# Hybrid mixer and MoE step on one core: the convolution state's load is issued later, the second gate's tiles are done in split products, the layer norm sums on VectorE, and VectorE's order in the mixer is laid out anew

## The chip, the cores and the metric

The kernel runs on one core of a Trainium2 chip. The metric is the device time of one execution in microseconds (us). Three executions of the kernel before took 702.01, 702.13 and 704.56 us; the median is 702.13 us. A further execution was profiled: 702.46 us, of which 700.6 us lie between its first and its last instruction.

The engines are called as the profile calls them: PE (TensorE), DVE (VectorE), ACT (ScalarE), POOL (GpSimd), SP (SyncE, which only issues transfers here). SPq, ACTq and so on are the transfers that an engine issues.

## The reference

One step of a decoder trunk on 272 prompt rows (16 meta tokens and 256 prompt tokens) and 8 sample sequences of 4 tokens: T = 304 tokens, 1024 channels.

```python
xn = rmsnorm(x, norm1_g)
u_x, u_y, c_v, c_g, g_rnn, g_conv = split(xn @ w_in)          # w_in is 1024 x 6144
xc  = causal_dwconv(u_x, state_rglru_conv, width 4)
r, i = sigmoid(blockdiag(xc, w_rg_a) + b_rg_a), sigmoid(blockdiag(xc, w_rg_i) + b_rg_i)
a = exp(-8 r softplus(-lambda));  h = scan(a, sqrt(1 - a*a) * i * xc, state_rglru_h)
rnn_out = (h * gelu(u_y)) @ w_rnn_proj
glu = c_v * sigmoid(c_g)
cc  = causal_dwconv(glu, state_conformer_conv, width 31)
conv_out = silu(layernorm(cc, conf_ln_g, conf_ln_b)) @ w_conv_proj
x = x + (sigmoid(g_rnn) * rnn_out + sigmoid(g_conv) * conv_out) @ w_out
x = x + moe(rmsnorm(x, norm2_g))                               # 4 groups x 8 experts, 2 of a group
y = rmsnorm(x, final_norm_g)
```

It returns y and the new states of the scan and of both convolutions.

## The kernel before

Everything up to `w_out` is the mixer; channels lie on the partitions, 128 at a time, so a tensor is 8 channel tiles (KT) of 304 tokens. A **tile** `(k, c)` is one 128 x 304 output of a 1024-row weight. There are 64, in this order: `cv 0, cg 0, ..., cv 7, cg 7` (the two halves of the GLU), then eight each of `ux`, `uy`, `gr`, `gc` (the two output gates), `rp` (`w_rnn_proj`) and `cp` (`w_conv_proj`). They cycle through four PSUM banks; a tile waits until the one four places ahead has been read (`tile_act` for ACT's, `glu_done` and `tile_dve` for DVE's). The weights come in blocks of 2 MB (four tiles) through four places in the buffer `ring`, loaded by SP when the tiles of the block four ahead are done (`load_block`).

Tiles up to `gc` are eight fp32 products each (L1426). Those of `rp` and `cp`, and `w_out` behind them, are **split products**: a weight half-block of two tiles is rounded by ACT into `w_hi` (`weight_high(u)`, L625), DVE subtracts to get `w_lo` in the weight's own place (`weight_low(u)`, L1009), the input is split likewise (`gel_hi`, `gel_lo`; `cc_hi`, `cc_lo`; `mrg_hi`, `mrg_lo`), and PE does three fp32r products for each of the eight input tiles (L1421). `w_hi` has three places (HI_SLOTS), so `weight_high(u)` waits for the two tiles of `u - 3`.

**Start.** SP issues x, half of the first weight block, eight small parameters and the rest of that block, then block 1. ACT issues five small parameter loads and, as fourth of six, the 0.96 MB `state_conformer_conv` into `crow` (L522; 1920 pieces of 512 bytes); then it computes the row norms. PE transposes the parameters (waits `par_in`), the convolution state (`conf_states`, waits `cst_in`) and the normalized x (L1386), whose copies into `xnT` let the first tile begin. DVE copies the transposed state into `glu` (L885) before its copies of `xnT`, then computes the softplus of lambda (`lam`).

**DVE's order** is written out by hand: `old_samples(c)` does the window products of the sample sequences with the old state (four products and a sum), `gate(c)` makes one channel tile of `glu` from the tiles `cv c` and `cg c`, `conv_prompts(c)` does the 30 taps (L952) of two channel tiles, `conv_rnn` the width-4 convolution, `variance` and `scans` the recurrence. Parts of one stand between taps of another (`between`). PE's `gates(c)` (the block-diagonal products, L1438) wait for `conv_rnn`.

**Layer norm.** The mean of `cc` over channels is eight fp32 products with a matrix of 1/1024, before tile `rp 1` (L1462); the mean of the squares is eight more, before `rp 5` (L1467). DVE and ACT subtract, square, take the root, normalize, apply silu and split.

After the mixer, 32 experts pass in order, each with its 3 MB of weights loaded, split and multiplied.

## Time and profile before

| | before |
|---|---|
| median of three executions | 702.13 us |
| profiled execution, of which its span | 702.46 us, 700.6 us |
| PE busy | 641.0 us, 91% |
| DVE busy | 513.2 us, 73% |
| ACT busy | 356.2 us, 51% |
| mean share of DMA engines in 380 to 700.6 us | 0.80 |

The times of the trace are from the start of the span. The profile counts an fp32 product as two MATMUL instructions and an fp32r product as one, so a tile of eight fp32 products is "x16" and one of split products is "x24". The clock granted to PE stands as a share of full speed, 1.00 or about 0.50.

### The profile page before, as it was taken

What the parts mean: (1) busy time and instruction counts of PE and PEld (TensorE: products, weight loads), DVE (VectorE), ACT (ScalarE), POOL (GpSimd) and SP (SyncE); (2) the same over time, 40 slices, a digit from 0 to 9 for tenths busy, and PEclk for the clock granted to TensorE, in tenths of its full rate; (3) what the DMA queues carried; (4) which work ended last, traced back from release to release, by engine and by line L of the source; (5) the groups of instructions that cost most, each with busy time, mean ns of one, the idle gap of its engine ahead of it and who ended that gap; (6) DMA issues with size and microseconds to landing.
All of it is one profiled execution on the core that took longest, in us unless ns stands there. A gap on an engine that the chain in (4) does not pass through costs nothing.

```text
span 700.6 us, 7972 instructions
## 1 busy us (share of the span) xinstructions
PE 641.0 (91%) x2872; PEld 468.4 (67%) x2872; DVE 513.2 (73%) x783; ACT 356.2 (51%) x511; POOL 81.7 (12%) x78
## 2 busy tenths in 40 slices
PE   4499999999999989999998899999999999999930
PEld 4366677777777779997788566666666666666610
DVE  0479999998861864864469888888888888888506
ACT  2121111147612304644355877777777777777522
POOL 1000000022240000020000031111111111111110
PEclk9699999999999999999999999999999999999985
DMA  9482615333333333504071889999999999997114
GB/s 226 158 292 48 220 42 199 121 120 121 120 121 120 121 121 120 153 2 181 1 303 58 340 330 363 361 359 375 369 370 366 377 374 368 357 372 270 37 64 156
DMA packets 45717, 150.20 MB, mean 214 GB/s; under 512 B 9990, under 2 KB 13302, under 8 KB 33062
## 3 DMA queue, kind: packets, MB, share of 16 engines
q1 hardware_dynamic: 38112, 144.56, 55.8%
q10 hardware_dynamic: 3974, 2.54, 1.4%
q0 software_dynamic: 3584, 2.50, 1.1%
q8 instruction: 25, 0.41, 0.2%
q14 instruction: 22, 0.18, 0.1%
HBM read 145.51 MB, written 15.02 MB: 229 GB/s over the span
## 4 chain that ended last, share of the span: by engine, by line
PE 68%; DVE 9%; ACT 2%; DMA 2%; issue 1%; SPq 0%; ACTq 0%; POOLq 0%; DVEq 0%
PE bank L1607 25%; PE bank L1632 14%; PE bank L1426 11%; PE bank L1421 7%; PE bank L1517 5%; DVE work L952 2%; PE bank L1574 2%; DMA ring<-expert_rows 1%; PE bank L1619 1%; PE bank L1489 1%; ACT work L674 1%; PE bank L1467 1%; PE bank L1462 1%; DVE work L976 1%; DVE x L1335 1%
## 5 line engine op out<-in xcount | busy, mean ns | idle before, releaser
L1426 PE MATMUL bank<-work,ring 128*128 128x304 f32 x768 | 198.7, 419 | 3.6 <-DVE work L912 2.7
L1426 PEld LDWEIGHTS bank<-work,ring 128*128 128x128 f32 x768 | 145.6, 190 | 54.8 <-DVE work L912 3.7
L1244 DVE TENSOR_TENSOR lo_gu<-ring,hi_gu 128x2048 fp32r<-128x2048 f32 x64 | 143.8, 2288 | 39.7 <-ACT hi_gu L762 39.7
L762 ACT ACTIVATE hi_gu<-ring 128x2048 fp32r<-128x2048 f32 x64 | 118.6, 1901 | 0.0
L952 DVE SCALAR_TENSOR_TENSOR work<-work,par 128x272 f32<-128x272 f32 x240 | 108.2, 524 | 0.4 <-ACT work L585 0.3
L1607 PE MATMUL bank<-hi_gu,xe_hi 128*96 128x512 f32 x256 | 102.4, 400 | 0.6 <-ACT work L786 0.6
L1607 PE MATMUL bank<-hi_gu,xe_lo 128*96 128x512 f32 x256 | 100.5, 393 | 0.0
L1607 PE MATMUL bank<-lo_gu,xe_hi 128*96 128x512 f32 x256 | 100.4, 392 | 0.0
L1632 PE MATMUL bank<-ring,windows 128*96 128x512 f32 x128 | 65.2, 590 | 0.0
L1009 DVE TENSOR_TENSOR w_lo<-ring,w_hi 128x2048 fp32r<-128x2048 f32 x12 | 28.0, 2341 | 35.4 <-ACT w_hi L625 35.4
L1607 PEld LDWEIGHTS bank<-lo_gu,xe_hi 128*96 128x96 f32 x256 | 41.3, 162 | 17.6
L1607 PEld LDWEIGHTS bank<-hi_gu,xe_hi 128*96 128x96 f32 x256 | 42.3, 165 | 16.2 <-ACT work L786 0.8
L1607 PEld LDWEIGHTS bank<-hi_gu,xe_lo 128*96 128x96 f32 x256 | 41.4, 162 | 15.4
L800 ACT ACTIVATE gate_weights<-bank,rs_col 96x256 f32<-96x256 f32 x32 | 15.1, 472 | 59.2 <-PE bank L1607 59.1
L494 POOL DMA_INDIRECT expert_rows<-outst,row_i x16 | 25.6, 1602 | 157.9 <-ACT outst L780 157.9
L625 ACT ACTIVATE w_hi<-ring 128x2048 fp32r<-128x2048 f32 x12 | 22.9, 1912 | 40.5 <-PE bank L1421 29.0
L1244 DVE TENSOR_TENSOR lo_dn<-ring,hi_dn 128x1024 fp32r<-128x1024 f32 x32 | 39.0, 1219 | 2.1 <-ACT hi_dn L767 2.1
L1632 PE MATMUL bank<-hi_dn,hT_hi 128*96 128x512 f32 x64 | 38.0, 594 | 2.5 <-ACT outst L780 1.5
L494 POOL DMA_INDIRECT expert_rows<-work,row_i x16 | 22.6, 1410 | 111.2 <-ACT work L780 111.2
L767 ACT ACTIVATE hi_dn<-ring 128x1024 fp32r<-128x1024 f32 x32 | 34.1, 1066 | 0.0
L565 ACT ACTIVATE ring<-bank 128x304 f32<-128x304 f32 x8 | 3.4, 424 | 58.0 <-PE bank L1426 58.0
L1244 DVE TENSOR_TENSOR xe_lo<-work,xe_hi 128x768 fp32r<-128x768 f32 x32 | 30.4, 949 | 1.0 <-issue 0.9
(271 smaller groups left out, 946.9 us busy)
## 6 DMA issues: line engine op xcount, KB each, us to landing
ring<-w_exp_gate SPq DMA_DIRECT2D x32, 1024.0 KB, 6.8
ring<-w_exp_up SPq DMA_DIRECT2D x32, 1024.0 KB, 9.2
ring<-w_exp_down SPq DMA_DIRECT2D x32, 1024.0 KB, 9.7
ring<-w_in SPq DMA_DIRECT2D x11, 2048.0 KB, 8.4
ring<-w_rnn_proj SPq DMA_DIRECT2D x2, 2048.0 KB, 7.9
ring<-w_conv_proj SPq DMA_DIRECT2D x2, 2048.0 KB, 7.9
ring<-w_out SPq DMA_DIRECT2D x2, 2048.0 KB, 7.9
ring<-w_in SPq DMA_DIRECT2D x2, 1024.0 KB, 13.3
```

Of the source, the lines that this page charges most:

```text
L494: nc.gpsimd.indirect_dma_start(out=rows, out_offset=bass.IndirectOffsetOnAxis(ap=row_i[0:C, e:e + 1], axis=0), in_=row_st[e % 2], in_offse ...
L625: nc.scalar.activation(hi, w, ACT.Copy).then_inc(whi_done, 1)
L762: nc.scalar.activation(hi_gu[e % 2][:, k], w_gu[s][:, k], ACT.Copy).then_inc(ehi_gu, 1)
L767: nc.scalar.activation(hi_dn[e % 2], w_dn[s][:, 0], ACT.Copy).then_inc(ehi_dn, 1)
L952: ins = vec.scalar_tensor_tensor(y, glu[:, ch, w:w + TP], pcw[:, w, ch:ch + 1], y, ALU.mult, ALU.add)
L1009: vec.tensor_tensor(part, value, as_f32(high), ALU.subtract).then_inc(lo_sem, 1)
L1244: vec.tensor_tensor(part, whole, as_f32(high), ALU.subtract).then_inc(out_done, 1)
L1421: ins = mm(bank[m % 4][:, 0:T], w[:, i, cols], xp[i], start=(i == 0 and j == 0), stop=(i == KT - 1 and j == 2))
L1426: ins = mm(bank[m % 4][:, 0:T], mix_w[b % MIX_SLOTS][:, i, (c % MB) * P:(c % MB + 1) * P], xnT[:, i], start=(i == 0), stop=(i == KT - 1))
L1517: ins = mm(bank[q][0:ROWS[t]], xp[:, c, tok], w[:, i], start=(c == 0 and j == 0), stop=(c == KT - 1 and j == 2))
L1607: ins = mm(bank[b][0:C], xp[b][:, k], w[:, k], start=(k == 0 and j == 0), stop=(k == KT - 1 and j == 2))
L1632: ins = mm(bank[4 + n][0:C], hp, w[:, at], start=(j == 0), stop=(j == 3))
```

## The change

- The load of `state_conformer_conv` moves on ACT from its fourth transfer to behind the row norms' square root. PE transposes the state after tile 0 instead of before the transposes of x, and DVE copies it into `glu` behind `lam` instead of before `xnT`.
- The eight `gc` tiles become split products: `first_split` and `first_tile` begin at `gc`, so there are four more half-blocks, and the unit numbers of all later ones grow by four. ACT makes `xn_hi`, DVE `xn_lo` (in the place of `xnT`).
- The layer norm's sums over the eight channel tiles are two `tensor_reduce` on DVE (`csum`), each followed by one fp32 product: the first before `gc 7`, the second before `rp 3`. Subtraction and square are one instruction each instead of two.
- `old_samples`, `gate` and the taps stand in another order, and the split and `rp` steps behind them as well.

```diff
--- before.py
+++ after.py
...
+        xn_lo = chan(rounded("xn_lo", "work", 0, KT * T))
...
+        xn_hi = [rounded(f"xn_hi{c}", *(("gate_weights", 2 * KT * P - (HB - c) * T) if c < HB else
+                                        ("ring", MIX_SLOTS * BLOCK_WORDS + (c - HB) * T)), T) for c in range(KT)]
...
+        csum = cv4[0][:, 0:T]
...
-        first_split, first_tile = blocks.index(("rp", 0)), tile_at["rp", 0]
+        first_split, first_tile = blocks.index(("gc", 0)), tile_at["gc", 0]
         WO_UNIT = 2 * (blocks.index(("wo", 0)) - first_split)
...
-            act.dma_start(crow[0:120], a["state_conformer_conv"][0].rearrange("s r (c p) -> (s r c) p", p=P)
-                          .rearrange("(i q) p -> q i p", i=16)).then_inc(cst_in, 16)
             act.dma_start(prow[64:72, 3], a["norm2_g"][0].rearrange("(c p) -> c p", p=P)).then_inc(par_in, 16)
             act.dma_start(prow[0:96, 4:6], a["state_rglru_conv"][0].rearrange("s r (c p) -> (s r c) p", p=P)
                           .rearrange("(i q) p -> q i p", i=2)).then_inc(par_in, 16)
...
             nc.scalar.activation(stat[:, 3:6], stat[:, 3:6], ACT.Sqrt).then_inc(rs_done, 1)
+            act.dma_start(crow[0:120], a["state_conformer_conv"][0].rearrange("s r (c p) -> (s r c) p", p=P)
+                          .rearrange("(i q) p -> q i p", i=16)).then_inc(cst_in, 16)
 
...
+                if (k, c) == ("gr", 0):
+                    weight_high(0)
+                    weight_high(1)
+                if (k, c) == ("gr", 1):
+                    act.wait_ge(gate_mm, KT)
+                    for i in range(KT):
+                        nc.scalar.activation(xn_hi[i], xnT[:, i], ACT.Copy).then_inc(xhi_done, 1)
+                if (k, c) == ("gr", 3):
+                    weight_high(2)
                 if k == "gc" and c in (1, 3, 5):
-                    weight_high(c // 2)
+                    weight_high(c // 2 + HI_SLOTS)
...
-            weight_high(3)
-            for q in range(2):
-                half = slice(q * HB, q * HB + HB)
-                act.wait_ge(cen_done, q + 1)
-                nc.scalar.activation(sq[:, half], cc[:, half], ACT.Square).then_inc(sq_done, 1)
-            weight_high(4)
+            act.wait_ge(cen_done, 1)
+            nc.scalar.activation(sq, cc, ACT.Square).then_inc(sq_done, 1)
+            weight_high(6)
             act.wait_ge(var_done, 1)
             nc.scalar.activation(sq[:, 0], sq[:, 0], ACT.Sqrt).then_inc(std_done, 1)
-            weight_high(5)
+            weight_high(7)
...
-            weight_high(6)
+                if c == HB:
+                    weight_high(8)
+            weight_high(9)
+            weight_high(10)
...
@@ -878,11 +892,6 @@
             dve.wait_ge(rst_T, 1)
             vec.tensor_copy(state_cols(ux, UXP, UXS)[:, :, 0:RW - 1],
                             bank[1][:, 0:192].rearrange("p (s r c) -> p s r c", s=NS, r=RW - 1)).then_inc(rst_done, 1)
-            for s in range(NS):
-                dve.wait_ge(cst_T, s // 2 + 1)
-                at = GLP + s * GLS
-                b = bank[4 + s // 2][:, 240 * (s % 2):240 * (s % 2) + 240]
-                vec.tensor_copy(glu[:, :, at:at + CW - 1], b.rearrange("p (r c) -> p c r", c=KT)).then_inc(cst_done, 1)
...
+            for s in range(NS):
+                dve.wait_ge(cst_T, s // 2 + 1)
+                at = GLP + s * GLS
+                b = bank[4 + s // 2][:, 240 * (s % 2):240 * (s % 2) + 240]
+                vec.tensor_copy(glu[:, :, at:at + CW - 1], b.rearrange("p (r c) -> p c r", c=KT)).then_inc(cst_done, 1)
...
                     dve.wait_ge(cstep, 2 * c)
+                else:
+                    dve.wait_ge(cst_done, NS)
...
-            for c in range(3):
-                old_samples(c)
+            old_samples(0)
+            old_samples(1)
             gate(0)
-            for c in range(3, 6):
-                old_samples(c)
+            old_samples(2)
+            old_samples(3)
             gate(1)
-            conv_prompts(0, between={4: lambda: old_samples(6), 5: lambda: gate(2), 10: lambda: old_samples(7),
-                                     13: lambda: gate(3), 22: lambda: gate(4)})
-            conv_prompts(2, between={1: lambda: gate(5), 10: lambda: gate(6), 18: lambda: gate(7), 24: new_samples})
+            old_samples(4)
+            old_samples(5)
+            gate(2)
+            conv_prompts(0, between={10: lambda: gate(3), 12: lambda: old_samples(6), 16: lambda: gate(4),
+                                     20: lambda: old_samples(7), 23: lambda: gate(5)})
+            conv_prompts(2, between={2: lambda: gate(6), 12: lambda: gate(7), 24: new_samples})
...
-            conv_prompts(6, between={12: lambda: weight_low(0), 18: lambda: weight_low(1), 24: lambda: weight_low(2)})
+            def tokens_low():
+
+                dve.wait_ge(tile_mm, first_tile)
+                for c in range(KT):
+                    low(xn_lo[:, c], xnT[:, c], xn_hi[c], xhi_done, xlo_done, c)
+
+            conv_prompts(6, between={6: lambda: weight_low(0), 10: lambda: weight_low(1), 16: lambda: weight_low(2),
+                                     22: tokens_low})
             vec.memset(spare, 1.0).then_inc(conv_done, 1)
             for c in range(KT):
                 low(gel_lo[:, c], gel[:, c], gel_hi[:, c], ghi_done, glo_done, c)
+
+            for i in range(KT):
+                dve.wait_ge(tap_done[i % 2], (i // 2 + 1) * (CW - 1))
+            dve.wait_ge(smp_done, 1 + 2 * TS)
+            vec.tensor_reduce(csum, cc.rearrange("p c n -> p n c"), AX_X, ALU.add).then_inc(sum_done, 1)
...
+            weight_low(3)
+            weight_low(4)
+            dve.wait_ge(mean_mm, 1)
+            vec.tensor_tensor(cc, cc, bank[4][:, 0:T].unsqueeze(1).broadcast_to([P, KT, T]), ALU.subtract)\
+               .then_inc(cen_done, 1)
+            weight_low(5)
+            dve.wait_ge(sq_done, 1)
+            vec.tensor_reduce(csum, sq.rearrange("p c n -> p n c"), AX_X, ALU.add).then_inc(sum_done, 1)
+            weight_low(6)
             tile("rp", 0)
-            dve.wait_ge(mean_mm, 1)
-            for q in range(2):
-                half = slice(q * HB, q * HB + HB)
-                vec.tensor_tensor(cc[:, half], cc[:, half], bank[4][:, 0:T].unsqueeze(1).broadcast_to([P, HB, T]), ALU.subtract)\
-                   .then_inc(cen_done, 1)
             tile("rp", 1)
-            weight_low(3)
-            tile("rp", 2)
-            tile("rp", 3)
-            tile("rp", 4)
             dve.wait_ge(var_mm, 1)
             vec.tensor_scalar(sq[:, 0], bank[5][:, 0:T], EPS, None, ALU.add).then_inc(var_done, 1)
             dve.wait_ge(std_done, 1)
             step(vec.reciprocal(sq[:, 0], sq[:, 0]))
             for c in range(KT):
                 vec.tensor_tensor(cc[:, c], cc[:, c], sq[:, 0], ALU.mult).then_inc(nrm_done, 1)
-            tile("rp", 5)
-            weight_low(4)
-            tile("rp", 6)
+            tile("rp", 2)
+            tile("rp", 3)
+            weight_low(7)
+            tile("rp", 4)
...
             for c in range(KT):
                 low(cc_lo[:, c], cc[:, c], cc_hi[:, c], chi_done, clo_done, c)
-                if c == 3:
-                    tile("rp", 7)
-            weight_low(5)
-            weight_low(6)
+                if c == 2:
+                    tile("rp", 5)
+                if c == HB:
+                    weight_low(8)
+                    tile("rp", 6)
+            tile("rp", 7)
+            weight_low(9)
+            weight_low(10)
             for c in range(KT):
...
-                    weight_low(c // 2 + 7)
...
-            pe.wait_ge(cst_in, 16)
-            for g in range(4):
-                conf_states(g)
...
                     x_hi, x_lo, ready = {"rp": (rows(gel_hi), rows(gel_lo), glo_done),
-                                         "cp": (rows(cc_hi), rows(cc_lo), clo_done)}[k]
+                                         "cp": (rows(cc_hi), rows(cc_lo), clo_done)}.get(k, (xn_hi, rows(xn_lo), xlo_done))
...
-                if (k, c) == ("rp", 1):
+                if (k, c) == ("gc", 7):
+                    pe.wait_ge(sum_done, 1)
                     pe.wait_ge(st_ev, 2)
-                    pe.wait_ge(smp_done, 1 + 2 * TS)
-                    for i in range(KT):
-                        pe.wait_ge(tap_done[i % 2], (i // 2 + 1) * (CW - 1))
-                        ins = mm(bank[4][:, 0:T], ones_d, cc[:, i], start=(i == 0), stop=(i == KT - 1))
-                    ins.then_inc(mean_mm, 1)
-                if (k, c) == ("rp", 5):
-                    for i in range(KT):
-                        pe.wait_ge(sq_done, i // HB + 1)
-                        ins = mm(bank[5][:, 0:T], ones_d, sq[:, i], start=(i == 0), stop=(i == KT - 1))
-                    ins.then_inc(var_mm, 1)
+                    mm(bank[4][:, 0:T], ones_d, csum, start=True, stop=True).then_inc(mean_mm, 1)
+                if (k, c) == ("rp", 3):
+                    pe.wait_ge(sum_done, 2)
+                    mm(bank[5][:, 0:T], ones_d, csum, start=True, stop=True).then_inc(var_mm, 1)
                 tile(m)
+                if m == 0:
+                    pe.wait_ge(cst_in, 16)
+                    for g in range(4):
+                        conf_states(g)
```

PE's instructions from its first products to the tiles. In the kernel before L1361 and L1364 transpose parameters, L1369 the convolution's state, L1386 x, and L1426 is a tile's product:

```order
L1364 MATMUL bank<-ident,ring 128x96 x2
L1369 MATMUL bank<-ident,ring 128x120 x16
L1386 MATMUL bank<-ident,ring 128x128 x2
L1386 MATMUL bank<-ident,ring 128x48
...
L1426 MATMUL bank<-work,ring 128x304 x176
```

In the changed kernel (L1406 is the state, L1419 x, L1459 a tile's product):

```order
L1401 MATMUL bank<-ident,ring 128x96 x2
L1419 MATMUL bank<-ident,ring 128x128 x2
L1419 MATMUL bank<-ident,ring 128x48
...
L1459 MATMUL bank<-work,ring 128x304 x8
L1406 MATMUL bank<-ident,ring 128x120 x16
L1459 MATMUL bank<-work,ring 128x304 x168
```

The state's 16 transposes moved behind the eight products of tile 0.

DVE's instructions from the last scan to the first `rp` tile, before (L952 is a tap, L1009 a low part, L1047 to L1054 copy states, L1004 reads a tile of `rp`):

```order
L995 SCALAR_TENSOR_TENSOR work<-ring 128x312 x4
L952 SCALAR_TENSOR_TENSOR work<-work,par 128x272 x30
L1009 TENSOR_TENSOR w_lo_62<-ring,w_hi_66 128x8x256
L952 SCALAR_TENSOR_TENSOR work<-work,par 128x272 x12
L1009 TENSOR_TENSOR w_lo_62<-ring,w_hi_67 128x8x256
...
L952 SCALAR_TENSOR_TENSOR work<-work,par 128x272 x14
L1042 MEMSET spare 128x1
L1009 TENSOR_TENSOR gel_lo<-work,gel_hi 128x304 x8
L1047 COPY outst<-bank 96x256
...
L1004 TENSOR_TENSOR work<-bank,work 128x304
```

In the changed kernel (L969 is a tap, L1026 a low part, L1076 the first sum, L1079 the first state copy, L1092 the subtraction of the mean, L1096 the second sum):

```order
L1012 SCALAR_TENSOR_TENSOR work<-ring 128x312 x4
L969 SCALAR_TENSOR_TENSOR work<-work,par 128x272 x18
L1026 TENSOR_TENSOR w_lo_65<-ring,w_hi_67 128x8x256
...
L969 SCALAR_TENSOR_TENSOR work<-work,par 128x272 x12
L1026 TENSOR_TENSOR xn_lo<-work,xn_hi_81 128x304
...
L969 SCALAR_TENSOR_TENSOR work<-work,par 128x272 x18
L1069 MEMSET spare 128x1
L1026 TENSOR_TENSOR gel_lo<-work,gel_hi 128x304 x8
L1076 TENSOR_REDUCE conv<-work 128x304
L1079 COPY outst<-bank 96x256
...
L1026 TENSOR_TENSOR w_lo_66<-ring,w_hi_67 128x8x256
L1026 TENSOR_TENSOR w_lo_63<-ring,w_hi_68 128x8x256
L1092 TENSOR_TENSOR work<-work,bank 128x2432
L1026 TENSOR_TENSOR w_lo_63<-ring,w_hi_69 128x8x256
L1096 TENSOR_REDUCE conv<-work 128x304
```

The first low part of a weight stands 12 taps earlier, the eight of `xn` stand before the last 18 taps, and between the low parts of `gel` and the two low parts of weights for `gc 6`, `gc 7` and `rp 0` there is now the first sum.

## Rows read from the trace of the kernel before

**Rows 1.** The page's first part: busy time of each engine.
```profile
PE 641.0 (91%) x2872; PEld 468.4 (67%) x2872; DVE 513.2 (73%) x783; ACT 356.2 (51%) x511; POOL 81.7 (12%) x78
```
**Rows 2.** Windows: length, busy PE, PEld, DVE, ACT, POOL, clock, DMA share, GB/s.
```profile
380.00:700.60 320.60, 289.53 (x1197) 188.90 (x1195) 239.95 (x211) 230.13 (x305) 48.39 (x33) 0.96 0.80 306
```
**Rows 3.** The chain that ended last: start, us, what.
```profile
157.36 1.47 DVE ring L983
...
213.73 24.58 PE bank L1426 x96
...
249.41 5.13 PE bank L1421 x24
254.54 4.09 PE bank L1462 x16
258.63 13.44 PE bank L1421 x96
...
314.75 15.29 PE bank L1517 x66
```
**Rows 4.** Timeline of the start: start, us, engine line op names shapes xcount [idle before <-releaser].
```profile
3.19 7.37 ACTq L524 DMA_DIRECT2D ring<-norm_g  x1
...
13.72 1.28 ACT L531 ACT_TABLE_LOAD   x1 [13.72 <-issue]
...
18.71 0.21 ACT L544 ACTIVATE stat<-stat 128x3 f32<-128x3 f32 x1 [0.23 <-DVE stat L867]
...
19.16 2.07 DVE L873 TENSOR_SCALAR ring<-x,stat 128x1024 f32<-128x1024 f32 x3
...
26.96 0.95 PE L1361 MATMUL bank<-ident,ring 96*128 96x96 f32 x4 [17.01 <-DMA ring<-state_rglru_conv]
...
28.03 3.38 PE L1369 MATMUL bank<-ident,ring 120*128 120x120 f32 x16
...
31.23 4.50 PE L1386 MATMUL bank<-ident,ring 128*128 128x128 f32 x24
...
36.65 23.52 PE L1426 MATMUL bank<-work,ring 128*128 128x304 f32 x91 [0.92 <-ACT work L549]
...
41.75 2.16 DVE L921 TENSOR_TENSOR windows<-work,par 128x248 f32<-128x248 f32 x4
```
**Rows 5.** Transfers of 0 to 30 us: queue with packets, MB, share; issue with us to landing.
```profile
q1 hardware_dynamic: 2608, 5.47, 61.6%
q10 hardware_dynamic: 2539, 1.26, 21.3%
...
ring<-w_in SPq DMA_DIRECT2D x1, 2048.0 KB, 20.1
ring<-state_conformer_conv ACTq DMA_DIRECT2D x1, 960.0 KB, 23.0
...
x<-x_sample SPq DMA_DIRECT2D x1, 128.0 KB, 9.6
```
**Rows 6.** Timeline of PE: the longer of its two stalls among the first tiles.
```profile
63.08 16.64 PE L1426 MATMUL bank<-work,ring 128*128 128x304 f32 x64 [1.64 <-DVE work L912]
```
**Rows 7.** Timeline of DVE and ACT behind the last scan.
```profile
187.34 17.10 DVE L952 SCALAR_TENSOR_TENSOR work<-work,par 128x272 f32<-128x272 f32 x30
224.21 2.29 DVE L1009 TENSOR_TENSOR w_lo<-ring,w_hi 128x2048 fp32r<-128x2048 f32 x1 [19.76 <-ACT w_hi L625]
226.42 5.04 DVE L952 SCALAR_TENSOR_TENSOR work<-work,par 128x272 f32<-128x272 f32 x12
...
234.56 0.80 ACT L643 ACTIVATE gel_hi<-work 128x304 fp32r<-128x304 f32 x2
```
**Rows 8.** Groups of DVE by shape: busy us, mean ns.
```profile
L925 DVE TENSOR_REDUCE work<-windows 128x32 f32<-128x992 f32 x8 | 9.5, 1186 | 0.3
...
L1112 DVE TENSOR_TENSOR halves<-x,halves 128x512 fp32r<-128x512 f32 x4 | 4.5, 1138 | 0.0
...
L1098 DVE TENSOR_TENSOR x<-bank,x 128x512 f32<-128x512 f32 x4 | 2.7, 685 | 4.2 <-PE bank L1517 4.2
```

More of the change, by code:

```diff
@@ L230, in trunk @@
         stat, spare = sb("stat", 21), sb("spare", 1)
-        (par_in, first_in, cst_in, wbd_in, router_in, g_in, consts, zeros, dconst, dstep, astep, pstep, rstep,
+        (xhi_done, xlo_done, par_in, first_in, cst_in, wbd_in, router_in, g_in, consts, zeros, dconst, dstep, astep, pstep, rstep,
          ss_done, ms_done, rs_done, xn_done, par_T, par_done, rst_T, rst_done, cst_T, cst_done, xT_done, xnT_done, xnT_act,
@@ L236, in trunk @@
          gate_mm, gate_act, dec_done, vsq_done, vrt_done, inp_done, scan_done, gelu_done, prod_done,
-         st_cp, st_T, st_ev, st_out, mean_mm, cen_done, sq_done, var_mm, var_done, std_done, nrm_done, silu_done,
+         st_cp, st_T, st_ev, st_out, mean_mm, cen_done, sq_done, sum_done, var_mm, var_done, std_done, nrm_done, silu_done,
          merged, wo_mm, x1_done, ss2_done, ms2_done, rs2_done, xT2_mm, pad_done, ss_half, xT2_act, xT2_dve,
@@ L243, in trunk @@
          y_out) = (sem(n) for n in (
-            "par_in first_in cst_in wbd_in router_in g_in consts zeros dconst dstep astep pstep rstep "
+            "xhi_done xlo_done par_in first_in cst_in wbd_in router_in g_in consts zeros dconst dstep astep pstep rstep "
             "ss_done ms_done rs_done xn_done par_T par_done rst_T rst_done cst_T cst_done xT_done xnT_done xnT_act "
@@ L247, in trunk @@
             "gate_mm gate_act dec_done vsq_done vrt_done inp_done scan_done gelu_done prod_done "
-            "st_cp st_T st_ev st_out mean_mm cen_done sq_done var_mm var_done std_done nrm_done silu_done "
+            "st_cp st_T st_ev st_out mean_mm cen_done sq_done sum_done var_mm var_done std_done nrm_done silu_done "
             "merged wo_mm x1_done ss2_done ms2_done rs2_done xT2_mm pad_done ss_half xT2_act xT2_dve "
@@ L701, in _ @@
             for c in range(1, KT + 1, 2):
-                weight_high(c // 2 + 7)
+                weight_high(c // 2 + 11)
                 for i in (c - 1, c):
@@ L705, in _ @@
                     nc.scalar.activation(mrg_hi[:, i], sgr[:, i], ACT.Copy).then_inc(mhi_done, 1)
-            weight_high(11)
+            weight_high(15)
             load_table(ACT.Sqrt)
@@ L1085, in _ @@
                 if c % 2:
-                    weight_low(c // 2 + 7)
+                    weight_low(c // 2 + 11)
                 if c >= 2:
@@ L1090, in _ @@
                 low(mrg_lo[:, c], sgr[:, c], mrg_hi[:, c], mhi_done, mlo_done, c)
-            weight_low(11)
+            weight_low(15)
             def residual(n, t):
```

## The prediction

> **What bounds the kernel now.** PE is busy 91% of the span [rows 1], so I read its gaps and the chain of waits, stage by stage. The timeline of the start comes first: PE transposes nothing until 26.96 us, when the last parameter lands, and its first tile starts at 36.65 [rows 4]. From there the chain runs over DVE up to 157.36 + 1.47 = 158.83 us [rows 3] (taps and recurrence; PE's gates wait for it), and PE stalls now and then for `gate`, 1.64 us at the longest [rows 6]. Then PE leads: `gc` from 213.73, `rp` from 249.41, `cp` up to 314.75, where `w_out` begins [rows 3]. In that stretch DVE had room: it stood 19.76 us before its first low part of a weight [rows 7]. From 380 us on the experts keep PE busy 289.5 of 320.6 us [rows 2]; nothing changes there, their loads start when mixer tiles end, and a gain before simply moves them. So the sum has two terms: how much earlier DVE's chain starts, and how much shorter `gc` to `cp` becomes.
>
> **The start.** The state's load fills ACT's queue: the tiny transfer behind it takes 7.37 us to issue, ACT computes only from 13.72, and the last parameter, two transfers behind, lands at 26.96 [rows 4]. Without it five small issues remain, done at about 4 us (estimate). What then sets the pace:
> - x. Its last part landed 9.6 us after its issue [rows 5], at 12.3 us. ACT's queue took 21.3% of 30 us x 16 engines for 2539 packets, 40 ns each; SP's took 61.6% for 2608, 113 ns each [rows 5]. The state's 1920 packets are 4.8 us of all engines; I take 1.8 of these out before x: 10.5 us. ACT and DVE needed 21.23 - 15.00 = 6.2 us from the table load to the end of the normalized x [rows 4]; two of the three squares (1 us each, estimate) now pass while x arrives, so it is ready at 10.5 + 4.2 = 14.7, the root at about 12.4.
> - Parameters. SP's eight stand behind x and half a block, 2.2 of 5.47 MB, or 7.4 of its 18.5 us; with ACT's other 619 packets (1.5 us), a start at 2.5 and about 2 us to land I take 14 us. Ends: 10.5 (with x) and 26.96 (no gain).
> - PE. 1.07 us of parameters [rows 4], about 1 us until DVE has copied them, then the 36.65 - 31.23 = 5.4 us of x less the 1 us that its first two channel tiles overlap: tile 0 from 20.5 to 24.6.
> - The state, issued at 12.4, is then the last. The same load took 23.0 us while ACT's queue served 2539 packets, of which it was 1920: 23.0 x 1920 / 2539 = 17.4 us. Two packets of 40 and 113 ns in turn on 16 engines give 9.6 ns x 1920 = 18.4. I take 17.6, landing at 30.0. Ends: inside tile 0 (by 24.6) and 12.4 + 23.0 = 35.4.
> - PE waits 5.4 us, transposes the state in 31.23 - 28.03 = 3.2 us [rows 4] and starts tile 1 at 33.2 instead of 36.65 + 4.09 = 40.7. Block 1, whose load took 20.1 us [rows 5] and was issued at 7.3, is there. DVE copies the last state 0.9 us later and begins `old_samples` at 34.1 instead of 41.75 [rows 4]: **7.6 us earlier**. `lam` (3.4 us) ends by then, hidden under the wait; if the state came early, up to 2 us of it would show.
>
> [...]
>
> **The order of `old_samples`, `gate` and taps.** The same instructions. Counting in tiles of 4.09 us from tile 1, each `gate` now stands before PE needs its bank, so the stalls (1.64 and a shorter one) go. But PE then waits that much at `gates(0)` for `conv_rnn`: DVE's chain is the same length, and the cost is 0. If DVE met a `gate` too soon it would lose at most 0.4 us each.
>
> **`gc` to `cp`.** All times here are on the clock of before; 7.6 comes off afterwards. On PE alone the change is large: a split tile takes 13.44 / 4 = 3.36 us against 4.09 (eight: 5.8), and two times eight sum products of 4.09 (there are two such rows) become two of 0.51 (7.2). But the order on DVE and ACT decides.
> - DVE from 187.34: 18 taps. POOL works beside it until 200, and the 30 taps took 17.10 instead of 12.5 [rows 7]; I put all of the 4.6 before 200, so the 18 end at 199.1. Then three low parts at 2.2 (starts follow each other 0.08 before an end) and 32 taps at 0.42 [rows 7], 20.0: DVE begins `xn_lo` at 219.1. ACT's `w_hi` and `xn_hi` are done by 199. PE was ready at 213.73 and waits 5.8.
> - `gc 0` takes 5.13 as the first `rp` tile did after its wait of 3 us (249.41 less 213.73 and eight tiles) [rows 3]: 224.7. `gc 1` to `5`: 241.5.
> - `gel_lo`. ACT makes the last two `gel_hi` behind its reading of `gc 4` (238.1), 0.4 + 0.8 [rows 7]: 239.3, `gel_lo` ends 239.8. Then the first sum, 1.7 us of state copies and one low part of 2.25 stand before `gc 6`.
> - The sum reads 2432 values with a stride of 304. Lower end: TENSOR_REDUCE took 1186 ns for 992 in a row [rows 8], so 2.9 us. The only strided pass over SBUF of which the trace has a twin is L1112, 1138 ns against 685 for 512 [rows 8], about 2.1 ns a value: 5.2 us. Upper end, with no row: twice that per value on top of the reduce, 8. I take 5.2, since the stride is the nearest likeness.
> - So the weights for `gc 6` come at 239.8 + 5.2 + 1.7 + 2.25 = 249.0; PE waits 7.5, `gc 6` takes 5.1 (to 254.1), mean product and `gc 7` 3.9: `rp` starts at 258.0 instead of 249.41, 8.6 us late.
> - `rp`. Before 5.13 + 7 x 3.36 + 2 x 4.09 = 36.8, to 286.3; now 8 x 3.36 + 0.5 = 27.4, to 285.4. The layer norm must keep up. Mean at 254.6; subtraction 2.7, square 2.3, second sum 5.2: 264.8; a low part and two `rp` tiles on DVE: 268; the product before `rp 3` at 268.1. From variance to the last `cc_lo` took 13.5 us before and gets one more weight split (1.9): 284. It fits with 1 us to spare.
> - `cp`. Before it ended at 314.75, 28.45 after `rp`, 1.5 of them waits for `cc_lo`. Now 8 x 3.37 = 27.0: 312.4. **Gain 2.3 us.**
>
> [...]
>
> **Sum.** 702.46 - 7.6 - 2.3 = 692.6 for an execution like the profiled one; its time lies 0.3 above the median, so **692.3 us**. Ends: the state's landing moves it by +5.4 to -5.4, the sums by -2.3 to about +4.6 (below).
>
> **Rivals.**
> - A. The state lands within tile 0. Tile 1 at 27.8: 5.4 us less, 687. For: block and x drain before, leaving room. [...]
> - B. The state takes 23.0 again, behind block 2 as well: 5.4 us more, 697.7.
> - C. DVE keeps up in `gc`, the PE arithmetic counts in full: 5.8 + 7.2 + 2.3 + 1.7 for the wait and slow tile before `rp` = 17, plus the start: 677.5. Against: the order on DVE, step by step above; the 19.76 us of room lie before the weights' split, but `gel_lo` and the sum stand after `gc 4`.
> - D. Slower: the sums are dearer than any row. The first moves `gc 6` one to one; the second, beyond 6.2 us, uses up the layer norm's spare 1 us and counts too. At r us each: 692.3 + 1 + 2 (r - 6.2). At 10.6 us (4.4 ns a value) the gain is gone; at 12.5 us it is 706. For: nothing measured has this stride. Against: the dearest strided row is 2.2 ns.
>
> **How the numbers follow.** Forecast 0.56 (its own range 688 to 697), A 0.14, B 0.12, C 0.04, D 0.10 (most of it with 7 to 11 us, 695 to 703), the rest unnamed. The range 684.5 to 700 takes in A and B with their own spread and leaves out C, half of D and the unnamed. A measurement here tells about 0.5%, 3.5 us, from no change: faster (under 698.6) 0.86, same 0.09, slower 0.05.
>
> **What would show it.** Tile 0 at 20 to 21 us, state transposes at 30, `old_samples` at 34; no stall among the first tiles, one of 2 us at the gates; PE idle some 6 us before `gc 0` and 7 before `gc 6`; TENSOR_REDUCE of about 5.2 us twice; no gap between `rp 7` and `cp 0`. It is wrong if tile 0 starts after 24 us, the state lands outside 27 to 33, or the sums are outside 4 to 6.2 us.

## The result, and the profile after

The changed kernel takes 693.5 us (median of 4 runs, 692.93 to 693.88) against 702.43 for the kernel before (4 runs, 702.01 to 704.56); the ratio is 0.9866, with a 95% interval of 0.9845 to 0.9888. 692.3 was predicted. The profiled execution took 693.58 us, with a span of 691.8.

The start first. The view is the timeline of the kernel after (start, us, engine line op names shapes xcount, and in brackets the idle time before with its releaser); it answers to [rows 4]. L1391 are products whose results nobody reads: 24 of them keep PE busy at the start.
```profile
1.58 7.74 PE L1391 MATMUL bank<-ident 128*128 128x128 f32 x48 [1.58 <-POOL ident L444]
...
12.93 0.34 ACTq L548 DMA_DIRECT2D ring<-state_conformer_conv  x1
...
15.48 0.95 PE L1398 MATMUL bank<-ident,ring 96*128 96x96 f32 x4 [6.17 <-DMA ring<-rg_lambda]
...
16.55 7.11 PE L1419 MATMUL bank<-ident,ring 128*128 128x128 f32 x24
24.58 6.97 PE L1459 MATMUL bank<-work,ring 128*128 128x304 f32 x16 [0.92 <-ACT work L554]
31.39 1.80 PE L1406 MATMUL bank<-ident,ring 120*128 120x120 f32 x16
33.03 17.31 PE L1459 MATMUL bank<-work,ring 128*128 128x304 f32 x67
...
34.72 2.16 DVE L938 TENSOR_TENSOR windows<-work,par 128x248 f32<-128x248 f32 x4
```
PE gets the parameters at 15.48 instead of 26.96 and DVE begins `old_samples` at 34.72 instead of 41.75: 7.03 us. But x's transposes take 7.11 us where they took 4.50, and tile 0 6.97 where one takes 4.09; nothing stands before the state's transposes. Tile 0's eight fp32 products stand there as x16. The windows of the same kernel say why (busy time of PE, PEld, DVE, ACT, POOL, then the granted clock, DMA share, GB/s):
```profile
10.00:15.00 5.00, 0.00 (x0) 0.00 (x0) 1.97 (x5) 2.39 (x5) 0.00 (x0) 0.79 1.05 337
15.00:20.00 5.00, 4.52 (x18) 2.87 (x18) 2.50 (x5) 0.51 (x1) 0.00 (x0) 0.50 1.06 357
20.00:25.00 5.00, 4.08 (x14) 2.31 (x14) 1.07 (x2) 1.95 (x5) 0.00 (x0) 0.50 1.03 200
25.00:30.00 5.00, 5.00 (x11) 3.30 (x11) 2.90 (x17) 2.58 (x3) 0.00 (x0) 0.51 1.22 340
30.00:35.00 5.00, 5.00 (x30) 4.10 (x30) 2.89 (x9) 0.00 (x0) 0.00 (x0) 1.00 0.62 224
```
The granted clock is 0.50 from 15 to 30 us, and 0.79 on average in the 5 us before; PE had stood idle for the 6.17 us before the parameters. In windows of 0.25 us from 5 to 40 us it is 1.00 or 0.50, here and in the kernel before, with other values only where it changes (0.72 and 0.64 here, 0.89 and 0.97 before); a value in between for 5 us is an average of the two. The state had been issued at 12.93 and, by the view of the transfers, took:
```profile
ring<-state_conformer_conv ACTq DMA_DIRECT2D x1, 960.0 KB, 16.4
```
It landed at 29.3, behind the slow tile 0.

Then `gc` to `cp`: first what PE waited for between 15 and 310 us (us in total, times, longest), then the chain that ended last (`gc 0` to `4`, `gc 6`, `w_out` and the group that is read below), which answers to [rows 3].
```profile
PE bank L1454 <- DVE w_lo L1026: 6.6, 1, 6.6
PE bank L1454 <- DVE xn_lo L1026: 6.2, 1, 6.2
...
PE bank L1471 <- DVE work L993: 2.5, 1, 2.5
```
```profile
212.90 19.16 PE bank L1454 x120
...
241.97 4.95 PE bank L1454 x24
...
304.95 19.48 PE bank L1549 x84
...
345.60 4.08 PE bank L1521 x24
```
PE waits 6.2 us for `xn_lo` before `gc 0`, 6.6 for the weight's low part before `gc 6`, and `w_out` begins at 304.95 instead of 314.75, 9.80 us earlier; 9.9 was predicted. The tiles behind these two waits are slow as well: the first five of `gc` take 19.16 us where five of 3.36 would take 16.8, with a granted clock of 0.50 in their first 4.8 us and 1.00 from there, and `gc 6` (x24, three fp32r products for each of eight input tiles) takes 4.95, at 0.70 on average. DVE's timeline shows what stood before that low part:
```profile
207.34 5.04 DVE L969 SCALAR_TENSOR_TENSOR work<-work,par 128x272 f32<-128x272 f32 x12
212.29 3.17 DVE L1026 TENSOR_TENSOR xn_lo<-work,xn_hi 128x304 fp32r<-128x304 f32 x8
215.37 7.51 DVE L969 SCALAR_TENSOR_TENSOR work<-work,par 128x272 f32<-128x272 f32 x18
...
224.63 0.86 DVE L1026 TENSOR_TENSOR gel_lo<-work,gel_hi 128x304 fp32r<-128x304 f32 x2 [1.56 <-ACT gel_hi L657]
...
231.34 0.86 DVE L1026 TENSOR_TENSOR gel_lo<-work,gel_hi 128x304 fp32r<-128x304 f32 x2 [4.29 <-ACT gel_hi L657]
...
233.67 4.38 DVE L1076 TENSOR_REDUCE conv<-work 128x304 f32<-128x2432 f32 x1
...
239.56 4.47 DVE L1026 TENSOR_TENSOR w_lo<-ring,w_hi 128x2048 fp32r<-128x2048 f32 x2
```
From 223 to 233 DVE stands 7.2 us idle before `gel_lo` in four waits (1.56, 0.69, 4.29, 0.69), and only then sums.

The spans differ by 8.8, not 9.8. The last 1.0 us goes in the routing stretch: the transposes of the second half of x take 4.08 us in the chain above, and in the kernel before, in the same view:
```profile
355.40 3.18 PE bank L1489 x24
```
The instructions are the same. The windows of 5 us that begin 40 us behind `w_out`'s start hold this group and show a lower granted clock (first before, then after):
```profile
354.75:359.75 5.00, 4.62 (x35) 4.14 (x35) 2.11 (x9) 3.74 (x8) 0.74 (x1) 0.92 0.97 370
```
```profile
344.95:349.95 5.00, 4.62 (x29) 4.04 (x29) 1.35 (x5) 3.74 (x8) 0.22 (x1) 0.74 1.00 365
```
The group is 0.9 of the 1.0 us. In the kernels below it took 3.18 to 4.32 us; in runs 5, 8, 9 and 12 it took 3.18, but twelve products of `w_out` that end some 5 us before it took 4.41 to 4.54 us instead of 2.98, and in run 1 both were slow. I found no reason for it, so I compare the kernels by `w_out`'s start as well as by their time.

### The profile page after: what moved, and what is told of

It reads as the page before. It is cut to its first block, busy times and chain, and to the rows that moved or that the text cites. A ratio compares the mean times of both kernels' runs of the same rounds, so it can differ in the third digit from the quotient of the medians.

```text
span 691.8 us, 8085 instructions
## 1 busy us (share of the span) xinstructions
PE 634.8 (92%) x2908; PEld 470.6 (68%) x2908; DVE 532.8 (77%) x796; ACT 365.4 (53%) x522; POOL 82.7 (12%) x78
## 4 chain that ended last, share of the span: by engine, by line
PE 61%; DVE 8%; DMA 2%; ACT 1%; issue 1%; SPq 0%; ACTq 0%; POOLq 0%; DVEq 0%
PE bank L1639 26%; PE bank L1664 14%; PE bank L1454 12%; PE bank L1549 5%; DVE work L969 3%; PE bank L1606 2%; DVE w_lo L1026 1%; DMA ring<-expert_rows 1%; PE bank L1521 1%; PE bank L1651 1%; DVE conv L1076 1%; DVE x L1372 1%; DMA expert_rows<-work,row_i 0%; DVE x L1362 0%; PE bank L1511 0%
## 5 line engine op out<-in xcount | busy, mean ns | idle before, releaser
L1459 PE MATMUL bank<-work,ring 128*128 128x304 f32 x640 | 169.1, 426 | 0.9 <-ACT work L554 0.9
L1459 PEld LDWEIGHTS bank<-work,ring 128*128 128x128 f32 x640 | 123.8, 194 | 44.7 <-issue 3.6
L969 DVE SCALAR_TENSOR_TENSOR work<-work,par 128x272 f32<-128x272 f32 x240 | 107.7, 523 | 0.2
L1639 PEld LDWEIGHTS bank<-lo_gu,xe_hi 128*96 128x96 f32 x256 | 41.3, 162 | 17.7
L1026 DVE TENSOR_TENSOR w_lo<-ring,w_hi 128x2048 fp32r<-128x2048 f32 x16 | 37.0, 2321 | 12.5 <-ACT w_hi L630 12.5
L630 ACT ACTIVATE w_hi<-ring 128x2048 fp32r<-128x2048 f32 x16 | 30.5, 1910 | 24.3 <-PE bank L1454 11.9
L1454 PE MATMUL bank<-xn_hi,w_hi 128*128 128x304 f32 x64 | 21.5, 335 | 12.8 <-DVE w_lo L1026 6.6
```

What stands on the lines that cost most here:

```text
L630: nc.scalar.activation(hi, w, ACT.Copy).then_inc(whi_done, 1)
L969: ins = vec.scalar_tensor_tensor(y, glu[:, ch, w:w + TP], pcw[:, w, ch:ch + 1], y, ALU.mult, ALU.add)
L1026: vec.tensor_tensor(part, value, as_f32(high), ALU.subtract).then_inc(lo_sem, 1)
L1454: ins = mm(bank[m % 4][:, 0:T], w[:, i, cols], xp[i], start=(i == 0 and j == 0), stop=(i == KT - 1 and j == 2))
L1459: ins = mm(bank[m % 4][:, 0:T], mix_w[b % MIX_SLOTS][:, i, (c % MB) * P:(c % MB + 1) * P], xnT[:, i], start=(i == 0), stop=(i == KT - 1))
L1639: ins = mm(bank[b][0:C], xp[b][:, k], w[:, k], start=(k == 0 and j == 0), stop=(k == KT - 1 and j == 2))
```

## The experiments

Theory 1: the start gives about 7 us; the single products for the norm sums pay; the split of the gate tiles pays nothing, because DVE's order turns its saving on PE into waits and slow tiles behind them. Against it: all gain is the start; or the split and the sums give what their arithmetic on PE says; or DVE's new order of the first stage counts. All times are medians of 5 or 6 runs, ratios are to the kernel before on the same chip (703.3, 704.5 and 703.7 us in the three groups of four). The intervals of the ratios reach 1.3 to 2 us to either side; where those of two kernels overlap, their times do not tell them apart, and the start of `w_out` in their profiles (one execution each) has to. It is not exact either: tile 0 took 5.76 to 7.35 us in the eight kernels that, like the changed one, have 24 empty products and the late state, so tile 1 begins between 31.8 and 33.6 us. The edits are shown shortened, in the kernel's names.

**1. The late state alone**, on the kernel before.
```diff
 ACT  sqrt(stat).then_inc(rs_done)
+ACT  dma_start(crow <- state_conformer_conv)
 PE   tile(0)
+PE   wait cst_in; conf_states(0..3)
 DVE  lam ...
+DVE  copies of the state; old_samples(0) waits for them
```


> The kernel before with one edit: the conformer state is issued behind the root, transposed behind tile 0 and copied behind lam. Theory 1 (the start gives about 7 us, gc to cp gives 2.3 to 2.8 more): 702.4 - 7.0 = 695.4 us, w_out begins at 307.7; the short stalls of PE for gate come back but are taken off its wait at gates(0). Rival R1 (all of the gain is the start, the split tiles and sums cancel): 693.5. Rival R2 (the old order of the gates needs the early state and costs as much as its stalls, 2.7): 698.

Measured: 696.08 us, 0.9888 [0.9863, 0.9912]; `w_out` begins at 308.07, 6.7 us earlier than before. PE's stalls for `gate` are 3.2 us in two, and at the first gates it waits 0.3 us, where the changed kernel has 2.5. R2 is out, and so is R1: 308.07 is 3.1 behind the changed kernel. In time the two are 2.6 us apart and their intervals overlap, so R1 is out by `w_out` alone.

**2. Sums on DVE, gate tiles not split**: the edit of run 1, and
```diff
-PE   rp 1, rp 5: 8 x mm(ones_d, cc[:, i]) / mm(ones_d, sq[:, i])
+DVE  tensor_reduce(csum, cc / sq)
+PE   rp 2, rp 5: mm(ones_d, csum)
```
with subtraction and square in one instruction each, as in the changed kernel.


> The late state and the two norm sums on DVE, while the gate tiles of the conv half (gc) stay one fp32 product each; the mean product stands before rp 2, the variance product before rp 5. Theory 1 (on PE the split tiles save 5.8 us, but DVE's order makes PE wait 6.2 us before gc 0 and 6.6 before gc 6, so the split costs more than it saves): two sums of eight products of 4.09 become two of 0.51, 7.2 us less than the late state alone: 695.4 - 7.2 = 688.2, up to 689.5 if the layer norm is late; faster than the changed kernel by 4 to 5. Rival R3 (the split tiles pay what their arithmetic says): 693.5 + 5.8 = 699.3.

Measured: **689.16 us, 0.9805 [0.9778, 0.9832]**, faster than the changed kernel. `w_out` begins at 300.17. The chain (start, us, what) from `gc` on:
```profile
206.02 24.58 PE bank L1429 x96
...
256.16 4.61 DVE conv L1072
...
275.64 24.53 PE bank L1424 x174
300.17 19.48 PE bank L1519 x84
```
The fp32 tiles of `gc` run without a stop. R3 (699.3) is refuted: the split costs 4.8 us at `w_out` (0.7 of it lie in the start: tile 1 begins at 32.34 here and at 33.03 in the changed kernel), where its arithmetic on PE saves 5.8.

**3. Split tiles, sums on PE**: the changed kernel with eight products at both places, and no `tensor_reduce`.
```diff
-DVE  tensor_reduce(csum, cc / sq)
-PE   gc 7, rp 3: mm(ones_d, csum)
+PE   gc 7, rp 3: 8 x mm(ones_d, cc[:, i]) / mm(ones_d, sq[:, i])
```


> The changed kernel with the two norm sums back on PE (eight fp32 products each, at the places of the single ones). Theory 1: without the first TENSOR_REDUCE (4.4 us) on DVE the low part for gc 6 comes 4.4 us earlier, so PE's wait of 6.6 falls to 2.2; mean and variance products add 3.6 each, the second reduce was not on the path: 693.5 - 4.4 + 3.6 + 3.6 = 696.3. Rival R4 (the sums on DVE are hidden and save their whole PE time): 693.5 + 7.2 = 700.7. Rival R5 (the sums cost DVE more than they save PE): under 693.

Measured: 695.12 us, 0.9881 [0.9857, 0.9905]; `w_out` at 308.15, 3.2 behind the changed kernel (2.8 expected). PE's wait before `gc 6`:
```profile
PE bank L1447 <- DVE w_lo L1026: 2.3, 1, 2.3
```
6.6 has become 2.3: the first sum on DVE moves `gc 6` one to one. R4 and R5 fall, by `w_out`; the interval of the time overlaps with that of the changed kernel. With the late state in all four, `w_out` begins at 308.07 with neither edit, 308.15 with the split, 300.17 with the sums, 304.95 with both. Runs 1 and 2 have DVE's old order of the first stage, run 3 and the changed kernel the new one; run 4 tests what that does. The sums alone are worth 7.9, but 1.2 of them lie before `gc`, in the start, and 1.5 in tile `rp 0`: behind the same wait of 2.93 us it took 4.92 us in run 1 and 3.4 in run 2, where the granted clock stayed at 1.00. That leaves 5.2 for the sums, 2 less than PE's arithmetic, and PE's two waits at the single products are 1.3 of these. The split alone is worth 0, and beside the sums it costs 4.8.

**4. DVE's old order of the first stage** in the changed kernel (`old_samples`, `gate` and taps, rows as in the kernel before).

> The changed kernel with DVE's order of old_samples, gate and taps as before. Theory 1: PE stalls for gate among the first tiles again (1.6 us and a shorter one), and its wait of 2.5 us at gates(0) shrinks by as much, since DVE's chain is the same length: 693.5, within 0.5. Rival R2: the stalls add up, 696.2.

Measured: 693.68 us, 0.9862 [0.9838, 0.9886], the same as the changed kernel. What PE waited for:
```profile
PE bank L1456 <- DVE work L927: 2.1, 1, 2.1
```
One stall of 2.1 us for `gate` is back, and the 2.5 us at `gates(0)` are gone. `w_out` begins at 305.76, 0.8 behind the changed kernel, since `gc 6` took 6.36 us behind its wait and not 4.95. In time this part of the change is worth nothing, as priced.

**5. DVE's low parts laid out anew** in the changed kernel.
```diff
-conv_prompts(6, ... 22: tokens_low)
+conv_prompts(6, ... 17: tokens_low)
-gel_lo; sum 1; state copies; w_lo 3; w_lo 4; mean subtracted; w_lo 5
+sum 1; state copies; w_lo 3; gel_lo 0..3; mean subtracted; w_lo 4; gel_lo 4..7; w_lo 5
-PE: mean product before gc 7, variance product before rp 3
+PE: mean product before gc 4, variance product before rp 2
```


> The changed kernel with DVE's work laid out so that PE need not wait: xn_lo five taps earlier (right behind gr's last tile, before which its place in memory is not free), the first sum and the state copies right behind the taps and before gel_lo, the low part of gc 6 and 7 before gel_lo, the mean product before gc 4, the variance product before rp 2. Theory 1 (the split's saving was lost to DVE's order, 6.2 + 6.6 us of waits and slow first tiles): gc 0 starts at 208 instead of 212.9, no wait before gc 6, w_out begins at 291 to 293 instead of 304.95, time 693.5 - 13 = 680.5. Rival R6 (another wait takes its place: the high part on ACT for gc 6, or the layer norm before cp 0): only the 5 us of gc 0 and some, 686 to 688. Rival R7 (the split tiles run into PE's own clock): above 690.

Measured: 687.41 us, 0.9762 [0.9737, 0.9788]; half of what I expected. What PE waited for, and windows (columns as above):
```profile
PE bank L1497 <- DVE outst L1080: 4.8, 1, 4.8
PE bank L1458 <- DVE xn_lo L1026: 2.1, 1, 2.1
PE bank L1500 <- DVE conv L1100: 0.6, 1, 0.6
```
```profile
220.00:225.00 5.00, 2.16 (x16) 1.92 (x14) 4.54 (x5) 2.80 (x4) 0.00 (x0) 1.00 0.34 95
225.00:230.00 5.00, 3.03 (x10) 2.72 (x11) 5.00 (x9) 0.11 (x1) 0.00 (x0) 0.55 0.86 326
230.00:235.00 5.00, 5.00 (x30) 5.00 (x29) 5.00 (x6) 1.11 (x3) 0.00 (x0) 0.77 0.00 0
```
`gc 0` starts at 206.97, 208 was expected; its wait fell from 6.2 to 2.1. The wait before `gc 6` went, and one at the mean product came in its place: I had let the taps end at 212, but 28 of them come behind `xn_lo` and end at 221.1, so the sum is ready only at 225.9 and the state copies behind it a little later. Behind the wait the granted clock is 0.55 and 0.77, and four tiles take 15.25 us instead of 13.4. The time is the one of R6, but the wait is neither of the two that it named.

**6. 52 instead of 24 empty products at the start** of the changed kernel.
```diff
-keep_clock(2, 24)
+keep_clock(2, 52)
```


> The changed kernel with 52 instead of 24 of the empty products that PE makes before the parameters land, so that it stays busy to about 15 us. Theory 2 (x's transposes took 7.1 us and tile 0 took 7.0 because the granted clock was 0.5 after PE had stood idle from 9.3 us): they take 4.5 and 4.1 again, tile 0 ends at 26 instead of 31.4, PE then waits for the state (landed at 29.3), transposes it in 1.8, tile 1 at 31.2 instead of 33.0, time 691.7. Rival R8 (the transfers set the pace, the clock does not matter): the same times of transposes and tile 0, 693.5. Rival R9: block 2, issued behind the transposes of x and so 3 us earlier, slows the state: tile 1 at 33, 693.5, but transposes 4.5.

Measured: 696.59 us, 0.9887 [0.9861, 0.9912], and `w_out` at 309.18, 4.2 behind the changed kernel. The two intervals of the time overlap, but run 7, on the same chip and with one edit more, is 6.8 us faster. Neither the theory nor a rival had a loss. PE's timeline:
```profile
16.56 4.55 PE L1419 MATMUL bank<-ident,ring 128*128 128x128 f32 x24
22.02 6.02 PE L1459 MATMUL bank<-work,ring 128*128 128x304 f32 x16 [0.92 <-ACT work L554]
33.52 3.46 PE L1406 MATMUL bank<-ident,ring 120*128 120x120 f32 x16 [5.48 <-DMA ring<-state_conformer_conv]
36.77 13.45 PE L1459 MATMUL bank<-work,ring 128*128 128x304 f32 x47
```
x's transposes take 4.55 us at a granted clock of 1.00 (15 to 21.1 us), so the clock explains their 7.11. Tile 0 was expected at 4.1 and takes 6.02: the granted clock is 0.72 in 20 to 25 us, though PE stood idle for only 0.81 us before the parameters and 0.92 us before the tile. It does not matter here, as PE waits for the state anyway. For block 2 is issued behind them, 2.5 us earlier, and the state now takes 20.5 us instead of 16.4. PE waits 5.48 us for it and transposes it at a lower clock (0.75 in 30 to 35 us, 0.57 in 35 to 40), in 3.46 us instead of 1.80. R9 named the mechanism and made it too small.

**7. The same, with block 2 held back until the state has landed.**
```diff
 if b == 2:
     sp.wait_ge(xT_done, KT)
+    sp.wait_ge(cst_in, 16)
```


> As the run with 52 empty products, and block 2 is issued only when the state has landed. If the state shares the DMA engines with block 2 from 21 us on, it lands at 27 to 28 instead of 29 to 31 and tile 1 begins at 29.5: 690. If it shares them with blocks 0 and 1 alone, nothing moves against the run with 52 products.

Measured: 689.79 us, 0.9797 [0.9772, 0.9822]. The state takes 14.6 us, tile 1 begins at 29.04, `w_out` at 301.06:
```profile
21.50 4.33 PE L1460 MATMUL bank<-work,ring 128*128 128x304 f32 x16 [0.92 <-ACT work L555]
27.35 1.86 PE L1407 MATMUL bank<-ident,ring 120*128 120x120 f32 x16 [1.51 <-DMA ring<-state_conformer_conv]
29.04 21.15 PE L1460 MATMUL bank<-work,ring 128*128 128x304 f32 x82
```
Tile 0 takes 4.33 us at a granted clock of 1.00. The edits of runs 6 and 7 differ by the transfer beside the state alone; in the traces the clock differs too, but in both tile 1 waits for the state, which lands at 33.5 and 27.3. ACT's own next transfer, the 832 KB of `out_cc_s`, is not what slows the state: ACT issues it at 23.70 us in the changed kernel, at 21.15 in run 6 and at 20.63 here, where the state is fastest.

**8. Sums over eight values side by side**, in the changed kernel: the same count, other values than the reference adds.
```diff
-tensor_reduce(csum, cc.rearrange("p c n -> p n c"))
+tensor_reduce(csum, cc.rearrange("p c n -> p (c n)").rearrange("p (n c) -> p n c", c=KT))
```


> The changed kernel with both sums over eight values that lie side by side (it adds other values than the reference does; count, source and destination are the same). Theory 3 (the stride of 304 values costs): each TENSOR_REDUCE takes 1.2 ns a value, 2.9 us, instead of 4.38 and 4.66; the first moves gc 6 by 1.5 us, the second is not on the path: 692.0. Rival: no difference, the row price of 1.2 ns does not hold at 2432 values: 4.4 us and 693.5.

Measured: 691.6 us, 0.983 [0.9802, 0.9858]. The groups of DVE by shape (busy us, mean ns), here and in the changed kernel:
```profile
L1077 DVE TENSOR_REDUCE conv<-work 128x304 f32<-128x2432 f32 x1 | 2.7, 2678 | 0.0
```
```profile
L1076 DVE TENSOR_REDUCE conv<-work 128x304 f32<-128x2432 f32 x1 | 4.4, 4381 | 0.0
```
`w_out` begins at 301.82, 3.1 before the changed kernel: 1.7 by the shorter wait before `gc 6` (4.9 us) and 1.15 by a shorter tile 0 (5.76 us), which has nothing to do with the edit; the intervals of the times overlap. The duration of the sums themselves is what this run shows: 1.1 ns a value side by side, 1.8 with the stride of 304.

**9. As run 5, mean product before `gc 6`.**

> As the run with the low parts laid out anew, with the mean product before gc 6 instead of gc 4. Theory 1: that run lost 4.8 us of PE's time waiting for the sum and the copies before gc 4 (the taps end at 221.1, not at 212 as assumed) and 1.8 us in slower tiles behind the wait. Both go: w_out begins at 292 to 293 instead of 298.6, time 687.4 - 6.3 = 681. Rival: the wait moves to gc 6 or to cp 0, 685 or more.

Measured: 682.63 us, 0.9704 [0.9681, 0.9726]; `w_out` at 294.19 (298.6 in run 5). The wait of 4.8 us and the slow tiles behind it are gone; a shorter one has come before `gc 6`, and the one of 2.1 us before `gc 0` stays:
```profile
PE bank L1458 <- DVE w_lo L1026: 2.1, 1, 2.1
```
Run 2 is this kernel's likeness without the split, and its `w_out` begins at 300.17. So with DVE's queue laid out for it the split is worth 6.0 us, about what its arithmetic gives (5.8), where in the changed kernel it cost 4.8.

**10. As run 9, with the start of run 7.** This kernel has the lowest time of all.

> The former together with 52 empty products and block 2 held back until the state has landed. The start gave 3.7 us (693.5 to 689.8) and is in another stretch, so the gains add: 681 - 3.7 = 677.3. Rival: DVE's chain, not PE, sets gc 0, and both count once: 679 to 681 again.

Measured: **679.28 us, 0.9656 [0.9636, 0.9676]**, `w_out` at 292.02. In time the start is worth 3.35 us here against 3.7 by itself; by `w_out` it is 2.2 against 3.9. It is all there at `gc 0` (205.31 instead of 208.76), but `gc 6` and `gc 7` then take 8.45 us instead of 6.7, at a granted clock of 0.85 and 0.81 in 225 to 235 us; in run 9 it is 1.00 there.

**11. Block 2 held back, with 24 empty products.**

> The changed kernel with block 2 held back until the state has landed, and 24 empty products as before. If only the two edits together help: tile 0 still ends at 31.4 on the slow clock, behind the state's landing, so tile 1 stays at 33.0 and the time at 693.5. If the hold alone is what helped: 690.

Measured: 693.07 us, 0.9849 [0.983, 0.9867]. The state takes 14.4 us, but PE's slow tile 0 ends at 31.1 all the same; nothing to gain (`w_out` at 304.22). In these runs the clock and the transfer pay only together: 696.59 us with the products alone, 693.07 with the hold alone, 689.79 with both, against 693.5.

**12. As run 10, with the state issued before the third square.**

> As the run with all edits, with the state issued before the third square, 1.4 us earlier than behind the root. If the DMA engines' work until then sets the landing and parameters are not delayed: PE's wait of 1.5 us before the state's transposes shrinks to about 0.3, 676. If the state's packets delay the parameters (15.5): nothing gained or 0.5 to 1 us lost.

Measured: 680.06 us, 0.9665 [0.9647, 0.9684]: not faster. Issued at 10.52, 2.3 us earlier, the state takes 18.1 us instead of 15.0 and lands later:
```profile
28.63 1.86 PE L1412 MATMUL bank<-ident,ring 120*128 120x120 f32 x16 [2.35 <-DMA ring<-state_conformer_conv]
```
The runs of the two overlap (679.6 to 680.87 against 678.83 to 680.77), so it is at best worth nothing.

## Why the prediction was right, and where it was not

- **The start, 7.6 us: right in sum (7.03), by luck: two steps were wrong and cancel.** "Tile 0 from 20.5 to 24.6" came out as 24.58 to 31.4. That meets my own sign of being wrong, tile 0 starting after 24 us. About 1.5 us of the later start are parameters that landed later (15.48, not 14); the rest, and 2.9 us in tile 0 itself, is the granted clock of 0.50, a term that I did not have. The rows had it: in [rows 4] the state's transposes take 3.38 us behind an idle of 17 us, nearly all at a granted clock of 0.50, and I took that as their price; at a granted clock of 1.00 they take 1.80. "PE waits 5.4 us" for the state never appeared, because the slow tile 0 filled it; run 6 shows a wait of that size (5.48 us), though with a state that took 20.5 us; in run 7 and 10, with tile 0 at its full speed, it is 1.51 and 1.87. Tile 1 began at 33.03; 33.2 was predicted, but as 30.0 (the state lands) and 3.2, and it came as 31.4 (tile 0 ends) and 1.8.
- **The state's transfer, 17.6 us: 16.4, landing at 29.3 instead of 30.0.** Rival B (23.0, behind block 2) did not come, but the runs show what decides it: 14.4 to 15.0 us with block 2 held back, 20.5 with block 2 issued 2.5 us earlier. Issued 2.3 us earlier itself, with block 2 held back, it took 18.1 (run 12). So in these runs its time moved with what the other queue had open. That the packets of the two queues go in turn was my estimate; none of these numbers shows their order. Rival A, and with it the early end of my range (-5.4), needed a landing inside a tile 0 of 4 us, by 24.6. No run shows that: with the late state the earliest landing is 27.3, in run 7, 1.5 us behind the end of its tile 0.
- **The order of the first stage, 0: right** (run 4). The wait at the gates came out as 2.5 us; 2 was predicted.
- **`gc` to `cp`, 2.3 us: 2.8.** The waits of 5.8 and 7.5 were 6.2 and 6.6, and 0.3 of the first is a slip of mine: 187.34 us, 18 taps of 12.5 / 30 us and the 4.6 beside POOL give 199.4 and not 199.1. The first five tiles took 19.16 us instead of 18.6, `gc 6` 4.95 instead of 5.1; the sums took 4.38 and 4.66 instead of 5.2, which accounts for the smaller second wait. The stride costs 0.7 ns a value and not the 0.9 that I took from L1112; the forecast was nearer than either bound.
- **The 1.2 us too few** are, in the profiles, 0.6 of the start less 0.5 of `gc` to `cp`, and the 1.0 us lost behind `w_out` at a lower granted clock, which no step of mine had. "Nothing changes there" was right for the instructions and not for the clock.
- **Rival C** (677.5, DVE keeps up) was the most instructive. The changed kernel is not it. Run 9 has the same start and another order on DVE, and between DVE's `old_samples` and `w_out` it gains 13.5 us. C names 17, or 17.7 if the wait before `rp` stands at the 3.0 of the rows and not at 2.3. The two waits of 2.1 us and one of 0.8 are still there. Run 10 comes to 679.3 with a faster start, which C did not have. Most of PE's arithmetic was there to be had; DVE's order kept it. **Rival D** needed sums of 10.6 us to undo the gain; they took 4.4 and 4.7.

## What to carry to other kernels

Where work is taken from the engine that leads and handed to another, the saving lasts only if the other engine's queue has its new work done by then: look in its timeline for idle time behind a wait and put the work there (DVE stood 7.2 us before `gel_lo` while the sum stood behind it). Try each part of a change alone, since a part can cost what another gains: without its split tiles the change was 4 us faster, and with them in a better order (run 9) 11 us. And when a stretch is sped up, follow the transfers that its end sets free; one that was hidden behind slow work may then be in the way.

## What the hardware showed that I had not expected

- Behind two waits of 6.17 and 4.8 us PE lost time a second time. With 6.17 us of idling before, the granted clock was 0.50 from 15 to 30 us, and 24 transposes took 7.11 us instead of 4.55; after 4.8 us in run 5 it was 0.55 over 5 us, and a single product of 304 columns took 1.35 us, where it took 0.67 in run 9 at a granted clock of 1.00. Behind a shorter wait some tiles were slow and some not: behind 2.93 us before `rp 0` the tile took 5.13 us in the kernel before, at a granted clock of 0.67, 4.92 in run 1, at 0.70, and 3.4 in run 2, at 1.00.
- More work on PE at the start put `w_out` 4.2 us later, by way of a transfer on another queue: 960 KB in pieces of 512 bytes took 16.4 us in the changed kernel, 20.5 with the next block of 2 MB issued 2.5 us earlier (run 6), and 14.4 with that block held back (run 11).
- A `TENSOR_REDUCE` of 2432 fp32 values took 2.68 us side by side and 4.38 and 4.66 us at a stride of 304 values.
